# Feature-major x in three token chunks for the first projection, with the norm taken on TensorE

## The reference

```python
h = rmsnorm(x, norm_mix_pre[l])      # y = x * rsqrt(mean(x*x) + 1e-6) * g
proj = h @ w_in[l]
q, k, v, u, g_attn, g_ssm = jnp.split(proj, SPLITS, axis=-1)
q = q.reshape(B, L, N_Q_HEADS, HEAD_DIM)    # 8 heads of 64: 512 columns, four tiles of 128
```

## Time and profile before

| | us |
|---|---|
| device time, median of 3 runs | 2033.12 (2032.86 to 2034.78) |
| profiled execution, span from first to last instruction | 2031.3 |
| PE busy in that span | 2006.7 (99%) |
| DVE busy | 1321.0 (65%) |
| ACT busy | 861.8 (42%) |
| POOL busy | 278.2 (14%) |

### The profile page before, as it was taken

How to read it: one execution, slowest core, us unless ns; L and a number is a source line. 1 busy time by engine, 2 the same in 40 slices (tenths; PEclk the granted TensorE clock), 3 DMA queues, 4 the chain that set the end, 5 groups by cost and what they waited for, 6 DMA issues and landing times.

```text
span 2031.3 us, 24399 instructions
## 1 busy us (share of the span) xinstructions
PE 2006.7 (99%) x9422; PEld 1664.3 (82%) x9422; DVE 1321.0 (65%) x1489; ACT 861.8 (42%) x1268; POOL 278.2 (14%) x521
## 2 busy tenths in 40 slices
PE   7999999999999999999999999999999999999998
PEld 6888888888888888888888888888888888888877
DVE  5337687848359777764656678674675757545886
ACT  5347776153224344433433544543445333442233
POOL 2576197000110000000000322100000000000001
PEclk9999999999999999999999999999999999999999
DMA  5643333677322534458655742213232111356413
GB/s 150 138 94 120 125 105 107 169 261 257 126 73 94 163 131 162 163 208 326 241 211 193 259 149 80 67 61 116 96 108 104 62 55 50 104 220 234 146 67 110
DMA packets 198614, 289.74 MB, mean 143 GB/s; under 512 B 28099, under 2 KB 125028, under 8 KB 198244
## 3 DMA queue, kind: packets, MB, share of 16 engines
q1 hardware_dynamic: 186576, 264.21, 38.9%
q10 hardware_dynamic: 11924, 23.98, 3.6%
HBM read 209.91 MB, written 77.07 MB: 141 GB/s over the span
## 4 chain that ended last, share of the span: by engine, by line
PE 93%; DVE 4%; issue 1%; ACT 1%; DMA 0%; POOL 0%; SPq 0%; POOLq 0%; ACTq 0%; DVEq 0%
PE A L2622 8%; PE A L2624 8%; PE A L2623 8%; PE X L2977 7%; PE X L2979 7%; PE X L2978 7%; PE A L2977 5%; PE A L2979 5%; PE A L2978 5%; PE X L3018 3%; PE X L3017 3%; PE X L3015 3%; PE A L3018 2%; PE A L3017 2%; PE A L3015 2%; PE X L2622 2%
## 5 line engine op out<-in xcount | busy, mean ns | idle before, releaser
L1760 DVE TENSOR_TENSOR WL<-raw,WH 128x1024 fp32r<-128x1024 f32 (+1 forms) x94 | 98.0, 1043 | 145.5 <-ACT WH L1128 145.1
L1128 ACT ACTIVATE WH<-raw 128x1024 fp32r<-128x1024 f32 (+1 forms) x94 | 80.4, 856 | 248.9 <-PE A L2624 150.3
L1774 DVE TENSOR_TENSOR WL<-S,WH 128x512 fp32r<-128x512 f32 x160 | 110.2, 690 | 115.7 <-ACT WH L1156 114.0
L1156 ACT ACTIVATE WH<-S 128x512 fp32r<-128x512 f32 x160 | 100.3, 627 | 151.2 <-PE X L2979 71.7
L2622 PE MATMUL A<-XH,WH 128*128 128x512 f32 x384 | 150.6, 392 | 1.3 <-DVE WL L1760 1.1
L1774 DVE TENSOR_TENSOR WL<-raw,WH 128x512 fp32r<-128x512 f32 x120 | 82.5, 688 | 103.4 <-ACT WH L1156 103.4
L2623 PE MATMUL A<-XL,WH 128*128 128x512 f32 x384 | 149.6, 390 | 0.0
L2624 PE MATMUL A<-XH,WL 128*128 128x512 f32 x384 | 149.6, 390 | 0.0
L2977 PE MATMUL X<-TH,WH 128*128 128x512 f32 x344 | 134.0, 390 | 0.3 <-DVE Y L2100 0.3
L2978 PE MATMUL X<-TL,WH 128*128 128x512 f32 x344 | 133.8, 389 | 0.0
L2979 PE MATMUL X<-TH,WL 128*128 128x512 f32 x344 | 133.8, 389 | 0.0
(11 more groups left out here) (609 smaller groups left out, 5395.7 us busy)
## 6 DMA issues: line engine op xcount, KB each, us to landing
raw<-in_w_in SPq DMA_DIRECT2D x47, 1024.0 KB, 5.2
ring<-a_scr SPq DMA_DIRECT2D x26, 1024.0 KB, 9.1
ring<-in_w_ff_out SPq DMA_DIRECT2D x26, 1024.0 KB, 7.7
raw<-in_w_ff_in SPq DMA_DIRECT2D x16, 1024.0 KB, 7.9
a_scr<-SB SPq DMA_DIRECT2D x16, 1024.0 KB, 6.4
g_scr<-stage SPq DMA_DIRECT2D x24, 512.0 KB, 3.6
g_scr<-gst ACTq DMA_DIRECT2D x32, 256.0 KB, 3.4
x_scr<-xr ACTq DMA_DIRECT2D x16, 512.0 KB, 2.6
```

The lines of the kernel that those rows point to most:

```text
L1156: A(seven_home(WH, p, j), seven_weights(p, j), ACT.Copy).then_inc(w_hi, 1)
L1760: TT(unit_home(WL[:, r, 0:kb, :], key), unit_of(raw[:, SLOT[p], 0:kb, :], key, i), unit_home(WH[:, r, 0:kb, :], key).bitcast(f32), ALU.sub ...
L1774: TT(seven_home(WL, p, j), seven_weights(p, j), seven_home(WH, p, j).bitcast(f32), ALU.subtract).then_inc(w_lo, 1)
```

## The change

The host hands over x transposed (feature-major) and cut into token chunks of 256, 256 and 512 (`x_t0` to `x_t2`), the q weights tile by tile (`w_q_t`, 4 KB a partition), and the norm's gain as a column for each block of 128 features (`gain`). x lands in `XT[n]` in eight pieces (`PIECES`: four of two feature blocks for chunk 0, two of four blocks for chunks 1 and 2).

- Norm: ACT squares each piece (L1205). For chunks 1 and 2 DVE adds four feature blocks into one (`squares_sum`, L1870 and L1871). PE multiplies the squares, as float32 weights, with a column of ones (`mean_squares`, L2746), DVE adds the epsilon (`x_mean`), POOL raises to -1/2 (`x_rstd`), PE spreads the result over the partitions by products with the identity (`scale_rows`, L2756), and DVE multiplies x with gain and this row, one instruction for each feature block (`x_scale`, L1858).
- ACT then copies the high part (`x_high`, L1213) and DVE subtracts for the low part (`x_low`, L1864). No token tile is turned on PE.
- The four q tiles run chunk by chunk (`q_pass`, L2769) in X0, X1, A0 and A1 at once. All four are complete only at the end. Chunks 0 and 1 have products of 256 columns, chunk 2 of 512. `brow` and `ct` come after all of them.
- q weights have homes of their own for tiles 2 and 3 (`WQH`, `WQL`), and all four low parts are made by POOL (L3273).
- Ten products of ones with ones stand at PE's start. `bsel`, `rel` and `sink` are issued by SP behind x.

```diff
-pair("q", 4, 2)
+pair("q", 4)
-FILLS = [(("t", m), ("X0", "X1", "A0", "A1")[m if m < 4 else 2 + m % 2]) for m in range(MT)]
-FILLS += [(("q", 0), "X0"), (("q", 1), "X1"), (("q", 2), "A0"), (("brow", 0), "X1"), (("q", 3), "A1"),
+CHUNK_AT = (0, 256, 512, 1024)
+X_LOWS, CHUNK_ENDS = 6, (3, 5, 7)
+X_SCALED = {i: n + 1 for n, i in enumerate((0, 1, 2, 4, 6))}
+FILLS = [(key, "A1b") for n in range(3) for key in (("mc", n), ("ms", n))]
+FILLS += [(("q", 0), "X0"), (("q", 1), "X1"), (("q", 2), "A0"), (("q", 3), "A1"), (("brow", 0), "X1"),
           (("ct", 0), "X0"), (("ct", 1), "X1"), (("kv", 0), "A0"), (("kv", 1), "A1"), (("u", 0), "A0"),
...
+            for i in range(4):
+                x_piece(i)
+            q_tile(0)
+            sp.dma_start(gain, io["mix_pre_t"]).then_inc(pre1_in, 16)
+            q_tile(1)
+            for i in (4, 5):
+                x_piece(i)
+            q_tile(2)
+            q_tile(3)
+            for i in (6, 7):
+                x_piece(i)
...
+            def x_square(i):
+                n, ks = PIECES[i]
+                act.wait_ge(x_in[i], 16)
+                if i == 6:
+                    filled(act, ("mc", 1))
+                A(SQ[n][:, ks, :], XT[n][:, ks, :], ACT.Square, scale=1.0 / 32).then_inc(sq0, 1)
...
-            hi(("q", 2))
             q_high(0)
-            hi(("q", 3))
             q_high(1)
             hi(("kv", 0))
             q_high(2)
+            q_high(3)
             filled(act, ("brow", 0))
...
-            q_high(3)
...
+            def x_scale(i):
+                n, ks = PIECES[i]
+                width = CHUNK_AT[n + 1] - CHUNK_AT[n]
+                filled(dve, ("ms", n))
+                for k in range(ks.start, ks.stop):
+                    ins = STT(XT[n][:, k, :], XT[n][:, k, :], gain[:, k:k + 1], psum(("ms", n))[:, 0:width], ALU.mult, ALU.mult)
+                ins.then_inc(evicted["A1b"] if i in CHUNK_ENDS else x_scaled, 1)
...
+            def mean_squares(n, ks):
+                begin(("mc", n))
+                for k in ks:
...
+                    for t in range((CHUNK_AT[n + 1] - CHUNK_AT[n]) // P):
+                        last = mm(psum(("mc", n))[:, t:t + 1], SQ[n][:, k, t * P:(t + 1) * P], ones[:, 0:1], start=(k == 0 and t == 0),
+                                  stop=(k == ks[-1]), skip_group_check=True)
+                end(last, ("mc", n))
...
+            for i in range(10):
+                mm(psum(("mc", 0))[:, 0:P], ones[:], ones[:], start=True, stop=True)
+            mean_squares(0, range(KD))
+            scale_rows(0)
...
+            mean_squares(1, (0, 4))
+            for t in (2, 3):
+                pe.wait_ge(w_hi, UNIT["q", t] + 1)
+                q_pass(t, 0, "hh", opens=True)
+                q_pass(t, 0, "hl")
+                pe.wait_ge(w_lo, UNIT["q", t] + 1)
+                q_pass(t, 0, "lh", closes=True)
+                if t == 2:
+                    scale_rows(1)
+            for t in range(4):
+                if t == 0:
+                    pe.wait_ge(xt_hi, 6)
+                q_pass(t, 1, "hh", opens=True)
+                q_pass(t, 1, "lh")
+                if t == 1:
+                    mean_squares(2, (0, 4))
+                if t == 2:
+                    scale_rows(2)
+            pe.wait_ge(x_lows, 4)
+            for t in range(4):
+                q_pass(t, 1, "hl", closes=True)
...
+            pe.wait_ge(x_lows, 6)
+            for t in range(4):
+                end(q_pass(t, 2, "hl", closes=True), ("q", t))
...
+            x_rstd(0)
+            for t in range(3):
+                q_low_weights(t)
+            x_rstd(1)
+            q_low_weights(3)
+            x_rstd(2)
```

More of the change, by code:

```diff
@@ L106 @@
         PANEL_OF[_key] = (_p, _i)
-        if _key[0] not in WHOLE:
+        if _key[0] not in WHOLE and _key not in OWN_HOME:
             RING[_key] = len(RING_KEYS)
@@ new lines, in squares_sum @@
+            def squares_sum(n, half):
+                dve.wait_ge(sq0, 2 * n + half + 3)
+                S = SQ[n][:, 4 * half:4 * half + 4, :]
+                link(TT(S[:, 0:2, :], S[:, 0:2, :], S[:, 2:4, :], ALU.add))
+                TT(S[:, 0:1, :], S[:, 0:1, :], S[:, 1:2, :], ALU.add).then_inc(sq_sum, 1)
+            x_mean(0)
+            dve.wait_ge(pre1_in, 16)
+            for i in range(4):
+                x_scale(i)
+            x_low(0, 0)
+            x_low(0, 1)
+            squares_sum(1, 0)
@@ new lines, in scale_rows, with q_weights @@
+            def scale_rows(n):
+                begin(("ms", n))
+                pe.wait_ge(rstd_made, RSTD["x", n])
+                for t in range((CHUNK_AT[n + 1] - CHUNK_AT[n]) // P):
+                    m = CHUNK_AT[n] // P + t
+                    last = mm(psum(("ms", n))[:, t * P:(t + 1) * P], fr0[:, m:m + 1].to_broadcast([P, P]), ident[:], start=(t == 0),
+                              stop=True, skip_group_check=True)
+                end(last, ("ms", n))
+            def q_weights(t):
+                return q_home(WH, WQH, t), q_home(WL, WQL, t)
@@ new lines, in q_pass @@
+            def q_pass(t, n, what, ks=range(KD), opens=False, closes=False):
+                high, low = q_weights(t)
+                weights, moving = dict(hh=(high, XH), lh=(low, XH), hl=(high, XL))[what]
+                dst = psum(("q", t))[:, CHUNK_AT[n]:CHUNK_AT[n + 1]]
+                for k in ks:
+                    last = mm(dst, weights[:, k, :], xh_part(moving, n, k), start=opens and n != 1 and k == 0,
+                              stop=closes and k == KD - 1, skip_group_check=True)
+                return last
@@ new lines, in _ @@
+            pe.wait_ge(w_lo, UNIT["q", 1] + 1)
+            q_pass(1, 0, "lh")
+            pe.wait_ge(x_lows, 2)
+            for t in range(2):
+                q_pass(t, 0, "hl", closes=True)
+            mean_squares(1, (0, 4))
[7 more added lines that the diff above has]
+                    scale_rows(1)
@@ new lines, in _ @@
+            for t in range(4):
[11 more added lines that the diff above has]
+            for t in range(4):
+                for half in range(2):
+                    ks = range(4 * half, 4 * half + 4)
+                    if t == 0:
+                        pe.wait_ge(xt_hi, 7 + half)
+                    q_pass(t, 2, "hh", ks, opens=True)
+                    q_pass(t, 2, "lh", ks)
@@ L3364, in shape_constants, with laid_out @@
             "bucket_rows": bucket_rows(), "window_scale": window}
+def laid_out(inputs):
+    x = np.asarray(inputs["x"])[0].T.reshape(KD, P, SEQ).transpose(1, 0, 2)
+    q = np.asarray(inputs["w_in"])[0, :, 0:HEADS * HD].reshape(KD, P, KV, HEADS // KV, HD)
+    more = {f"x_t{n}": x[:, :, CHUNK_AT[n]:CHUNK_AT[n + 1]] for n in range(3)}
+    more["w_q_t"] = q.transpose(3, 1, 0, 2, 4).reshape(4, P, KD, P)
+    more["mix_pre_t"] = np.asarray(inputs["norm_mix_pre"])[0].reshape(KD, P).T
+    return {name: np.ascontiguousarray(a) for name, a in more.items()}
 def kernel(**inputs):
```

233 lines of the change are left out of this document (112 added, 121 removed).

## The result

The changed kernel takes 2042.38 us (median of 5 runs, 2040.83 to 2045.41), the kernel before beside it 2033.12 (5 runs, 2032.74 to 2034.78): a ratio of 1.0046, 95% interval 1.0036 to 1.0057. It is 9.3 us slower, where 1.1 was forecast, and lies outside the range.

What follows compares the result with a forecast made beforehand. PE was taken as the bound, busy 2006.7 of 2031.3 us. An earlier start, eaten by added products, waits and the hand-over, put `kv` 0 1.1 us later: 2033.12 + 1.1 = 2034.2 us, range 2030.0 to 2038.5.

Steps and rivals of the forecast that it cites:

- step 4: Waits inside the q chunks: 1.1 us in chunk 0, 1.3 before chunk 1, none for chunk 2; slow PE 0.5.
- rival C: PE at half speed for 5 us from the first q product and 5 us behind `ct`: 2038.7, chance 0.17.
- step 5: Sum for the q tiles: start, products, added work and waits put the last q product at 63.25 us, before 66.29.
- step 1: The start: x pieces, squares, sums, mean, power and scaling give the first q product at 11.6 us, 5.7 earlier.
- Step 2: The q products: 96 of 512 columns take 21.7 us, 192 of 256 columns at 0.117 take 22.5; restarts 0.8.
- the rival that the order itself is slow: Set against the theories after the measurement: the chunk-by-chunk order with 256-column products is slow; no size or chance given.
- POOL's low parts: Low parts of q weights on POOL: 2.1 us each, up to 2.9 if DVE holds it up; cost to PE nothing.
- the other waits: PE waits for scaled x: 1.3 us before chunk 1, nothing taken before chunk 2, up to 1.
- T: The time of the last q product, forecast at 63.25 us.
- Step 6: Hand-over to `kv`: `ct`'s second half waits for ACT's eviction of `brow`; `kv` 0 at 68.15, 1.1 us later than before.
- Step 7: Behind the hand-over: `kv` panel has 4.9 us of cover, `brow` store and bias load cost nothing; the end moves by 1.1.
- Each microsecond there should arrive at the end as one: Any shift in the start of `kv` 0 moves the program's end equally; unequal shifts would show the prediction wrong.

Runs made afterwards that it cites:

- e6_no_contention: Changed kernel with the low parts of q weights 2 and 3 on DVE instead of POOL, q tile 1's high half earlier on ACT: 2039.97 us, ratio 1.0035.
- e10_wide_mean: e8_all with the sixteen products summing chunk 0's squares 128 columns wide instead of one: 2029.07 us, ratio 0.9981.
- e7_lows_and_busy: e6_no_contention with products of ones spread out: eight ahead, two behind the sums, eight behind the scaling matrix: 2040.23 us, ratio 1.0036.
- e1_handover: Changed kernel with `brow` between chunks 0 and 1, q tiles ending 2, 0, 3, 1, and `kv` 0 directly behind them, before `ct`: 2044.10 us, ratio 1.0054.
- e5_late_store: e1_handover with `brow`'s 1.5 MB store moved behind the last q eviction: 2034.30 us, ratio 1.0008.
- e8_all: e5_late_store and e7_lows_and_busy together, with chunk 1's scaling products eight products earlier: 2031.14 us, ratio 0.9993.
- e11_wide_only: Changed kernel with one edit, chunk 0's sums of squares 128 columns wide instead of one: 2040.32 us, ratio 1.0039.
- e3_busy_ct: Changed kernel with eleven products of ones between the halves of `ct`, where PE waits for `brow`: 2043.23 us, ratio 1.0044.
- e4_no_warm: Changed kernel without the ten products of ones at its start: 2043.80 us, ratio 1.0053.

## Why the prediction was wrong

**The step that failed is the last sentence of step 4: "Slow PE in the first 4 us of q products: half a microsecond, more in rival C".** The mechanism was named and given away at 0.17, on the ground that no row after a gap inside the kernel shows a slow product. That was an argument from absence: before, no gap in the middle was as long as the one the change was about to make. In the changed kernel the clock is low from 9.3 to 19.6 us and again from 74.2 to 77.6. The cost of the first stretch in chunk 0 is 8.59 - 6.44 = 2.15 us (48 products, in e6_no_contention at the lower clock and from 12.47 to 18.91 in e10_wide_mean at the full one; e7_lows_and_busy took 5.8). The scaling matrix takes 1.19 for 0.68, 0.5 more; the second costs 1.6. Together that is 4.3 where the sum had 0.5. In step 5's sum chunk 0's first half is only 1.0 over; the slow products seem to cover waits and restarts (1.1 and 0.8) that were counted beside them, which is argued and not shown. Rival C had the right places; it priced 2.5 and 2.5. Its own 2038.7 was short by the items below: the rest of the lateness is step 1's queue of sums (1.2) and small terms. The rule of the Trainium skill that stood beside it ("TensorE: Matmul & The Clock Gate", section "HAM oscillation — how this bites in real kernels") speaks of idling between bursts. The trace agrees at `ct`: 0.54 behind the 2.40 us wait. The first fall isn't of that kind, since PE is listed as busy from 1.11 until the clock falls at 9.3.

The other steps:

- *Step 1, first q product at 11.6:* 13.45. The squares were ready nearly as forecast (7.47 for 7.3), but only four products were put behind them. In fact all sixteen stood in PE's queue behind the products of ones, which end at 5.54, and took 3.8 us at 0.24 each: the sums ended near 9.3 instead of 8.1. The power took 0.72 for 0.57, the scaling matrix 1.19 for 0.7. So the forecast was 1.85 too early, of which 1.2 are the queue and 0.5 the clock, under the scaling matrix.
- *Step 2, the products of 256 columns:* 0.120 a step in chunk 1 against 0.117. Right, and the rival that the order itself is slow falls: in e10_wide_mean the same order beats the kernel before.
- *Step 4, POOL's low parts, "nothing":* right for PE's wait on them, wrong for DVE. In step 4 only POOL was thought to be held up. DVE's addition of two operands in SBUF waited out POOL's subtraction: 2.88 for 0.68. The rule stands in the Trainium skill, "SBUF — State Buffer", section "SBUF: two separate sides": a DVE operation with two SBUF inputs and a GpSimd one that reads SBUF exclude each other for a whole instruction. The trace agrees: the held addition ended 0.55 behind POOL's row. It cost about 0.9 us (e6_no_contention).
- *Step 4, the other waits:* 1.53 before chunk 1 against 1.3, nothing but 0.33 before chunk 2 against nothing. Right.
- *Step 5, T = 63.25:* 68.6. Of the 5.4, 1.85 are the start, 1.0 chunk 0's first half (8.97 for 8.0), 0.4 the steps, 0.7 two short waits not in the sum (0.39 and 0.33), 0.2 chunk 1, 0.3 one-column products; about 0.9 in small restarts isn't placed.
- *Step 6, `kv` 0 at T + 4.9:* T + 5.1, by the waits foreseen. What it did not count is that this gap starts a slow stretch of its own, although rival C said so.
- *Step 7:* right for the panel: it was issued at 47.95, and ACT had it when it asked (67.50 behind the q evictions, no wait for a DMA). It was the cover that e1_handover used up.

"Each microsecond there should arrive at the end as one" did not hold as written, and the prediction named that as a sign of being wrong: the start of `kv` 0 moved by 6.6, the end of the program by 7.6. Between them stand the second slow stretch (1.6 more) and shorter waits further on (1.2 less). The median difference of 9.3 is larger because the profiled execution was the changed kernel's fastest.

In sum, the hand-over at `ct` with what it triggers costs 8 us (e5_late_store, intervals well apart). Taking the held DVE away gives 0.9 in the trace and 2.4 in the medians (e6_no_contention). Keeping the clock up at the start gives 2.1 once the other two are gone (e8_all to e10_wide_mean; 1.7 by the differences to the kernel before), and nothing that the trace shows while DVE is still held (e11_wide_only). Together these are 11 to 12.5 of the 13.1 between the changed kernel and e10_wide_mean. Without them the change is no longer a loss: e10_wide_mean is 3.8 us faster than the kernel before, of which its trace gives 2.2 to the start. What stays open is what in an execution decides how early the clock falls: the changed kernel's runs lie 4.6 us apart, and the profile shows one of them.

## What to carry to other kernels

A start that is made shorter by giving PE less to do has to be priced at the lower clock, from the first gap or scrap of work until well into the products that follow. A wait in the middle costs its length and then the slow products behind it, so let something useful stand there: here one reordering at a hand-over was worth 8 us, all the work on the start together 5 (e5_late_store to e10_wide_mean). Before a store or a subtraction is moved to "where nobody waits", look at what else goes over the same queues and which engine pairs exclude each other at that time.

## What the runs showed that was not expected

- PE can be listed as busy without a break and still lose its clock: e8_all has 5.0 us of one-column products back to back, and the granted clock is 0.50 from 7.5 us; e1_handover has no idle time since 1.11, and it falls at 8.6. With 128 columns a product the same place reads 1.00.
- A one-column product takes 0.24 as two instructions and 0.43 at the lower clock. PE's weight loads take 3.94 us beside 3.81 of products in the changed kernel, so it seems to go by its weight load. 128 columns cost next to nothing there: 3.87 (e10_wide_mean) and 4.14 (e11_wide_only) against 3.81 us for sixteen.
- The granted clock of the trace can't be trusted ahead of its first change. In e3_busy_ct it reads 1.00 from 10 to 18 us while the one-column products took 6.83/16 = 0.43 each, as in e4_no_warm. The durations tell the level; the slow transposes of the earlier trace rows under a reading of 1.00 fit this.
- A 1.5 MB store on ACT's queue stretched the issue of small loads on SP from 4.88 and 6.70 to 11.40 and 12.50 us, although the store itself was issued in 1.27; moved behind the last q eviction, it left them at 4.49 and 5.82.
- A change in one stage moved a wait 90 us further on: 1.14 for `WL` at 161 us before, 0.31 in the changed kernel, none with the new hand-over.
